# A second feature pass as seven quadrant products, with its input combined ahead of time

## The reference, cut to what matters

```python
def first_block(x, ...):                      # 2048 tokens, 1024 channels
    mixed = concat([y * silu(z) for y, z in branches])    # 1280 wide
    return x + mixed @ w_out                  # 1280 x 1024

def second_block(x, ...):
    xn = rms_norm(x, norm_g) * (1.0 + sc_x) + sh_x
    p = xn @ w_in                             # 1024 x 3072
    f_in, f_gate, q, k, v, na_gate = split_cols(p, six of 512)
    q = rms_norm(heads(q), q_norm_g)          # over each head's 64 channels
    k = rms_norm(heads(k), k_norm_g)
    f_out = fourier(f_in) * silu(f_gate)
    na_out = neighbourhood_attention(q, k, v, ...) * silu(na_gate)
    return x + g_x * (concat([f_out, na_out]) @ w_out)
```

## Time and profile before

| what | value |
|---|---|
| median of three runs | 3404.44 us |
| profiled execution, its span | 3402.36 us, 3400.6 us |
| PE matmuls, busy | 3111.9 us (92%) |
| PE weight loads, busy | 2445.2 us (72%) |
| DVE, ACT, POOL busy | 1514.0, 941.8, 795.5 us |
| token pass, its matmuls L2166 | 1850.4 to 2112.0 us of the span |
| feature pass 2, its last matmul L691 | starts at 2692.6 us |
| DMA | 390.82 MB, mean 115 GB/s |

### The profile page before, as it was taken

How to read it: one execution, slowest core, us unless ns; L and a number is a source line. 1 busy time by engine, 2 the same in 40 slices (tenths; PEclk the granted TensorE clock), 3 DMA queues, 4 the chain that set the end, 5 groups by cost and what they waited for, 6 DMA issues and landing times. The chain is left out here.

```text
span 3400.6 us, 39668 instructions
## 1 busy us (share of the span) xinstructions
PE 3111.9 (92%) x14503; PEld 2445.2 (72%) x14503; DVE 1514.0 (45%) x2504; ACT 941.8 (28%) x1520; POOL 795.5 (23%) x842
## 2 busy tenths in 40 slices
PE   3799999999988999775998999899999898999899
PEld 2588887888876666553897877677888675666687
DVE  6643333042306666386455222476000145777633
ACT  4422212110112334342222234322011133555400
POOL 5322222111112222265342222011111041000111
PEclk7899999999998999778898999999999998999999
DMA  7534335122243341314102666323211235776475
GB/s 272 184 97 116 102 101 180 61 77 75 75 127 87 90 105 55 90 47 97 43 26 82 200 185 208 109 112 123 74 74 74 99 102 134 155 158 142 112 199 148
DMA packets 325559, 390.82 MB, mean 115 GB/s; under 512 B 93879, under 2 KB 260264, under 8 KB 310696
## 3 DMA queue, kind: packets, MB, share of 16 engines
q1 hardware_dynamic: 320692, 387.11, 39.9%
q10 hardware_dynamic: 4704, 1.59, 0.2%
HBM read 256.77 MB, written 135.79 MB: 115 GB/s over the span
## 5 line engine op out<-in xcount | busy, mean ns | idle before, releaser
L691 PE MATMUL f_psum_out<-f_x_high,f_w_high 128*128 128x512 f32 (+1 forms) x1472 | 573.5, 390 | 18.8 <-DVE f_x_low L668 8.1
L691 PE MATMUL f_psum_out<-f_x_low,f_w_high 128*128 128x512 f32 (+1 forms) x1472 | 569.0, 387 | 0.0
L691 PE MATMUL f_psum_out<-f_x_high,f_w_low 128*128 128x512 f32 (+1 forms) x1472 | 568.6, 386 | 0.0
L691 PEld LDWEIGHTS f_psum_out<-f_x_high,f_w_high 128*128 128x128 f32 x1472 | 279.1, 190 | 77.9 <-issue 15.0
L691 PEld LDWEIGHTS f_psum_out<-f_x_low,f_w_high 128*128 128x128 f32 x1472 | 278.9, 189 | 56.5 <-issue 1.7
L691 PEld LDWEIGHTS f_psum_out<-f_x_high,f_w_low 128*128 128x128 f32 x1472 | 278.9, 189 | 55.5
L1351 PE MATMUL nbr_psum_o<-nbr_probT,nbr_v 128*128 128x512 f32 (+3 forms) x576 | 235.8, 490 | 0.0
L683 POOL CAST f_w_high<-f_w 128x1024 fp32r<-128x1024 f32 x41 | 42.6, 1040 | 747.8 <-PE f_psum_out L691 550.5
L532 PE MATMUL p_psum_proj<-p_w_high,p_h_high 128*128 128x512 f32 x512 | 207.5, 405 | 7.4 <-issue 4.0
L532 PE MATMUL p_psum_proj<-p_w_low,p_h_high 128*128 128x512 f32 x512 | 202.1, 395 | 0.0
L532 PE MATMUL p_psum_proj<-p_w_high,p_h_low 128*128 128x512 f32 x512 | 202.1, 395 | 0.0
(11 more groups left out here) (541 smaller groups left out, 6134.0 us busy)
## 6 DMA issues: line engine op xcount, KB each, us to landing
f_w<-in_w_fm SPq DMA_DIRECT2D x45, 512.0 KB, 5.7
side_ada_w<-in_w_ada_rows SPq DMA_DIRECT2D x24, 512.0 KB, 5.7
scratch_qkmT<-p_qkT_out SPq DMA_DIRECT2D x32, 384.0 KB, 4.6
scratch_z1T<-f_out SPq DMA_DIRECT2D x10, 1024.0 KB, 4.8
p_z<-scratch_z1T SPq DMA_DIRECT2D x16, 640.0 KB, 6.6
p_xt<-in_x SPq DMA_DIRECT2D x16, 512.0 KB, 3.9
p_staging<-in_w_tok SPq DMA_DIRECT2D x8, 1024.0 KB, 8.0
scratch_hT<-p_h_slot SPq DMA_DIRECT2D x16, 512.0 KB, 3.3
```

The lines of the kernel that those rows point to most:

```text
L691: last = nc.tensor.matmul(self.p_out[b][:, n * BANK + lo:n * BANK + hi], self.w_parts[b][w_part][:, k, :], self.x_parts[x_part][:, n, k, l ...
```

## The change: what it does

**Quadrants.** The 1024 input channels and the output are cut in two each, and the tokens too: the even tiles form one half of the columns, the odd tiles the other. A pair of output blocks is a 2x2 matrix A of 128x512 quadrants, the input a 2x2 matrix B. A pair now needs seven products of quadrants (Winograd's form of Strassen's scheme) instead of eight. Four of the left operands are sums of weight quadrants (`add_weights`, POOL), four of the right operands are sums of input quadrants (`combine`). DVE adds the seven products to the four results (`merge`).

**Input.** The scratch tensor x2T becomes x2q, with the seven right operands side by side: three quadrants (`move`) and four combinations, which `combine` makes on POOL for each pair of tiles and SP stores in the pair that follows (`move_combined`); for the last pair DVE fills the slot and combines. `fill` now waits also until the combinations of the pair before are stored.

**Pass.** The tokens go in two halves of 1024, and each half walks the 12 pairs in the order `F2_ORDER`, 24 items in all. An item is 7 products of 4 channel blocks by three passes, 84 matmuls of 128x512, into six PSUM banks used in rotation; two banks are left for the sums of squares and v's transposes (`aside`). The seven right operands (1 MB each) are held for a half and loaded anew for the second. There is one buffer for each of the seven split left operands; it is refilled for the next item when its product is done. The weights of item n+2 are loaded as item n begins.

**Roots.** The sums of squares of two heads are two rows of 1024. They are stored to DRAM and loaded as 128x16, ACT takes the root, DVE the reciprocal, and they go by DRAM again to be broadcast over 64 partitions each (`spread_sums`).

**The edge.** Before the last pair of tiles, SP, ACT, POOL and DVE begin with item 0's weights and first operand; before the last tile with the next operands. The second to last tile is transposed inside the last tile's matmuls. PE makes products 0 to 5 of item 0 before the barrier.

```diff
+class QuadrantPass:
+    A11, A12, A22, S1, S2, S3, S4 = range(7)
+    B11, B21, B22, T1, T2, T3, T4 = range(7)
+    PRODUCTS = ((A11, B11), (S2, T2), (A12, B21), (S3, T3), (A22, T4), (S1, T1), (S4, B22))
+    N, HK, BANKS = 7, KB // 2, 6
...
+    def load_w(self, sp, n):
+        if n >= 2:
+            sp.wait_ge(self.a_ready, self.N * (n - 1))
...
+    def load_x(self, sp, half, i):
+        if half:
+            sp.wait_ge(self.prod_ready, self.N * (half * self.per_half - 1) + i + 1)
...
+    def add_weights(self, pool, n):
...
+        pool.wait_ge(self.w_in[n % 2], 16 * (n // 2 + 1))
+        pool.drain()
+        nc.gpsimd.tensor_tensor(s1, a21, a22, ALU.add)
+        nc.gpsimd.tensor_tensor(s3, a11, a21, ALU.subtract)
+        pool.drain()
+        nc.gpsimd.tensor_tensor(s2, s1, a11, ALU.subtract)
+        pool.drain()
+        nc.gpsimd.tensor_tensor(s4, a12, s2, ALU.subtract).then_inc(self.sums_ready, 1)
...
+    def round_w(self, act, n, i):
+        a = self.PRODUCTS[i][0]
+        if n:
+            act.wait_ge(self.prod_ready, self.N * (n - 1) + i + 1)
+        if a < self.S1:
+            act.wait_ge(self.w_in[n % 2], 16 * (n // 2 + 1))
+        else:
+            act.wait_ge(self.sums_ready, n + 1)
+        self.nc.scalar.activation(self.a_high[:, i], self.quadrant(n, a), ACT.Copy).then_inc(self.a_rounded, 1)
+    def rest_of_w(self, pool, n, i):
+        pool.wait_ge(self.a_rounded, self.N * n + i + 1)
+        self.nc.gpsimd.tensor_tensor(self.a_low[:, i], self.quadrant(n, self.PRODUCTS[i][0]), self.a_high[:, i], ALU.subtract)\
+            .then_inc(self.a_ready, 1)
...
+    def product(self, pe, n, i):
+        pe.wait_ge(self.a_ready, self.N * n + i + 1)
+        if n % self.per_half == 0:
+            pe.wait_ge(self.x_ready[i], n // self.per_half + 1)
+        if self.N * n + i >= self.BANKS:
+            pe.wait_ge(self.prod_free, self.N * n + i + 1 - self.BANKS)
...
+        for k in range(self.HK):
+            for at, (w_part, x_part) in enumerate(PASSES):
+                last = self.nc.tensor.matmul(self.bank(n, i), a_parts[w_part][:, i, k, :], x_parts[x_part][:, k, :],
+                                             start=(k == 0 and at == 0), stop=(k == self.HK - 1 and at == len(PASSES) - 1))
+        last.then_inc(self.prod_ready, 1)
...
+    def combine(eng, ops, j):
+        b11, b21, b12, b22 = (slot[b][:, k:k + HK] for b in range(2) for k in (0, HK))
+        t1, t2, t3, t4 = (combined[:, n] for n in range(4))
+        eng.wait_ge(combined_stored, 16 * (j + 1))
+        ops.tensor_tensor(t1, b12, b11, ALU.subtract)
+        ops.tensor_tensor(t3, b22, b12, ALU.subtract)
+        eng.drain()
+        ops.tensor_tensor(t2, b22, t1, ALU.subtract)
+        eng.drain()
+        ops.tensor_tensor(t4, t2, b21, ALU.subtract)
+        eng.drain().then_inc(combined_ready, 1)
...
+                if b == 0:
+                    sp.dma_start(d["x2q"][:, 0:KB, of_pair], slot[0][:]).then_inc(slot_stored[0], 16)
+                else:
+                    sp.dma_start(d["x2q"][:, KB:KB + HK, of_pair], slot[1][:, HK:]).then_inc(slot_stored[1], 16)
+            def move_combined(j):
+                wait_apart(sp, combined_ready, j + 1, taken)
+                sp.dma_start(d["x2q"][:, KB + HK:, bass.ds(j * P, P)], combined[:].rearrange("p s k c -> p (s k) c"))\
+                    .then_inc(combined_stored, 16)
...
+                if b == 1 and not second:
+                    move_combined(j - 1)
...
+            def begin_next():
+                sp.wait_ge(w_ready, MB)
                 for b in range(2):
-                    fp.load(sp, d["w_fm2"], 0, b)
-            def begin_next():
+                    sp.wait_ge(slot_stored[b], 16 * (NT // 4 + 1))
+                sp.wait_ge(combined_stored, 16 * (NT // 4 + 1))
+                fp.load_w(sp, 0)
+                fp.load_x(sp, 0, 0)
+            def go_on():
+                sp.wait_ge(mix_ready[1], PAIRS)
+                sp.wait_ge(o_ready, NT - 1)
+                fp.load_x(sp, 0, 1)
                 sp.wait_ge(slices_used, 1)
-                fp.load_input(sp, d["x2T"], 0, 2)
-                sp.wait_ge(x1_ready[1], PAIRS)
-                fp.load_input(sp, d["x2T"], 2, 3)
+                fp.load_x(sp, 0, 2)
+                fp.load_x(sp, 0, 3)
+                sp.wait_ge(slices_used, 2)
+                fp.load_x(sp, 0, 4)
+                fp.load_x(sp, 0, 5)
...
-            tiles(sp, tile, next_weights, begin_next)
+            tiles(sp, tile, begin_next, go_on)
+            sp.wait_ge(o_ready, NT)
+            fp.load_x(sp, 0, 6)
+            fp.load_w(sp, 1)
             move(PAIRS - 1, 1)
-            sp.wait_ge(slot_stored[0], 16 * (PAIRS + 1))
-            fp.load_input(sp, d["x2T"], 3, 4)
-            sp.wait_ge(slot_stored[1], 16 * (PAIRS + 1))
-            fp.load_input(sp, d["x2T"], 4, 5)
+            move_combined(PAIRS - 1)
...
+                    if last and b == 1 and k == TURN_AT:
+                        turn_x(NT - 2)
+                    if last and b == 1 and k in (SLICES_LENT - 1, 2 * SLICES_LENT - 1):
...
+            for i in range(fp.BANKS):
+                if i == 4:
+                    pe.wait_ge(x_filled, NT)
+                fp.product(pe, 0, i)
+                if i == 1:
+                    turn_x(NT - 1)
...
+                act.wait_ge(combined_stored, 16 * (j + 1))
...
             def begin_next():
-                for b in range(2):
-                    fp.round_first_weights(nc, act, b)
-                fp.round_input(nc, act, 0, 2)
+                fp.round_x(act, 0, 0)
+                for i in range(fp.N):
+                    fp.round_w(act, 0, i)
+            def go_on():
+                fp.round_x(act, 0, 1)
+                fill(PAIRS - 1, 0)
+                fp.round_x(act, 0, 2)
+                fp.round_x(act, 0, 3)
...
-            tiles(act, tile, before_last=begin_next)
-            fill(PAIRS - 1, 1)
-            fp.round_input(nc, act, 2)
+            tiles(act, tile, begin_next, go_on)
+            for i in range(4, fp.N):
+                fp.round_x(act, 0, i)
...
+                if b == 0 and not first:
+                    wait_apart(pool, x_filled, 2 * j, taken)
+                    combine(pool, nc.gpsimd, j - 1)
             def begin_next():
-                for b in range(2):
-                    fp.rest_of_first_weights(nc, pool, b)
+                fp.add_weights(pool, 0)
+                for i in range(fp.N):
+                    fp.rest_of_w(pool, 0, i)
...
-            tiles(pool, tile, before_last=begin_next)
+            tiles(pool, tile, begin_next)
...
+            def begin_next():
+                fp.rest_of_x(dve, nc.vector, 0, 0)
+            def go_on():
+                fp.rest_of_x(dve, nc.vector, 0, 1)
+                fp.rest_of_x(dve, nc.vector, 0, 2)
+            tiles(dve, tile, begin_next, go_on)
...
+            dve.wait_ge(xT_ready, NT)
+            dve.wait_ge(slot_stored[1], 16 * PAIRS)
+            dve.wait_ge(combined_stored, 16 * PAIRS)
+            for k in range(KB):
+                nc.vector.tensor_scalar(slot[1][:, k, :], p_x[:, k, :], g.scale_x[:, k:k + 1], g.shift_x[:, k:k + 1], ALU.mult, ALU.add)
+            dve.drain().then_inc(x_filled, 1)
+            dve.wait_ge(x_filled, NT)
+            combine(dve, nc.vector, PAIRS - 1)
+            for i in range(5, fp.N):
+                fp.rest_of_x(dve, nc.vector, 0, i)
...
+F2_ORDER = (0, 4, 1, 5, 2, 6, 3, 7, 8, 9, 10, 11)
...
+            def spread_sums(n):
+                at = 2 * among(n, "qk")
+                for b in (1, 0):
+                    sp.wait_ge(rows_ready[b], at // 2 + 1)
+                    sp.dma_start(d["rms_in"][at + b], work[b][0:2, :]).then_inc(rows_stored[b], 16)
+                for b in (1, 0):
+                    sp.wait_ge(rows_stored[b], 16 * (at // 2 + 1))
+                    sp.dma_start(spread[b][:], d["rms_in"][at + b].rearrange("h (q c) -> (h q) c", q=HD)).then_inc(spread_in[b], 16)
+                for b in (1, 0):
+                    sp.wait_ge(rms_ready[b], at // 2 + 1)
+                    sp.dma_start(d["rms_out"][at + b].rearrange("h (q c) -> (h q) c", q=HD), spread[b][:]).then_inc(rms_stored[b], 16)
+                for b in (1, 0):
+                    sp.wait_ge(rms_stored[b], 16 * (at // 2 + 1))
+                    for h in range(2):
+                        sp.dma_start(work[b][h * HD:(h + 1) * HD, :], d["rms_out"][at + b, h].partition_broadcast(HD)).then_inc(rms_in[b], 16)
...
+            for n in range(LAST + 1):
+                if n + 2 <= LAST:
+                    fp.load_w(sp, n + 2)
+                if kind(n - 1) == "qk":
+                    spread_sums(n - 1)
+                if kind(n - 1) in ("qk", "v"):
+                    store(n - 1)
+                if n == fp.per_half - 1:
+                    for i in range(N):
+                        fp.load_x(sp, 1, i)
+                if kind(n) in ("in", "gate"):
```

(57 more changed lines are left out.)

368 lines of the change are left out of this document (223 added, 145 removed).

## The result

| | before | changed |
|---|---|---|
| median, us | 3403.52 (8 runs) | 3414.27 (8 runs) |
| lowest and highest | 3399.15, 3406.69 | 3411.70, 3417.54 |
| span of the profiled execution | 3400.6 | 3415.8 |
| PE's first product after the barrier | 2153.34 | 2159.56 |
| last matmul of the pass starts | 2692.61 | 2707.08 |

The ratio is 1.0035, its interval 1.0024 to 1.0045: slower, where 3359 was forecast with 0.92 on faster. The last two rows of the table say where. From PE's resumption (its first product after the barrier) to the pass's last matmul it is 547.5 us now and was 539.3: 8.2 us more with 264 matmuls fewer. The forecast for the same stretch was -59.7 + 3.6 + 4 + 1 = -51.1. So 59.3 us are missing there; the edge came out as forecast (+6.2 for +6.8).

What follows compares the result with a forecast made beforehand. TensorE (PE) was taken as the bound, matmuls times pace in the feature pass. Terms -59.7 + 4 + 1 + 6.8 + 3.6 + 0 - 1 gave -45.3 us, so 3359 us against the median, range 3341 to 3388.

Steps and rivals of the forecast that it cites:

- The edge: Between token and feature pass: reordered queues idle PE about 9 and 17 us, so PE resumes after the barrier +6.8 us later.
- The matmuls removed: Feature pass after the barrier: 264 fewer matmuls at 0.226 us each, -59.7 us if PE stays fed.
- (D): Rival, products: one takes over 2.71 us though PE is fed, gain shrinks 1.6 us per 0.01; (D) and the rest 0.05.
- The roots by DRAM and the six banks: q and k items: the roots' chain frees PE's bank with 1 to 3 us cover; 0.5 us for each of eight, +4.
- (B): Rival, q and k items: chain of roots outruns the six banks; 3387, or 3400 with DVE late; chance 0.28.
- Feeding by POOL: Steady items: POOL's eleven instructions at 1.2 us (upper end 1.77) take about 14 to 17 us, beside PE's 19.0.
- (C): Rival, items: POOL becomes the bound above about 1.85 us per instruction, kernel slower from 2.05; chance 0.05, with similar stalls.
- POOL after the ones: Before item 1: POOL makes four sums and one low part, 6.3 us, while product 6 covers 2.7; +3.6 us.
- The second half's input: Item 11 onward: seven operands loaded anew, last low part about when PE wants it; +1 us, between 0 and 8.
- (A): Rival, edge: pair 6's combinations land early and the 17 us wait goes; about 3342 us, chance 0.12.
- The sum: Whole kernel: all terms give -45.3 us, 3357.1 from the profiled execution, 3359 against the median.

Runs made afterwards that it cites:

- experiment 8: Changed kernel with roots after product 3, merge 0 into u3, the reordered edge, and item 1's sums on POOL before the barrier: 3342.46 us, ratio 0.9836.
- Experiments 1 and 3: Each against the changed kernel: 1 moves roots and reciprocals from product 5 to product 3, 3365.20 us; 3 cuts POOL's low parts to 128 columns, 3361.71 us.
- experiments 6 and 7: Changed kernel, roots after product 3: 6 makes pair 6's combinations on DVE, stored earlier, 3353.89 us; 7 also puts tile 14's work first, 3346.11 us.
- experiment 2: Changed kernel without the sums' way by DRAM, roots and reciprocals (result differs): 3360.43 us in one run.

## Why the prediction was wrong, step by step

- **The matmuls removed, -59.7:** right. Products run at 0.226 to 0.23 us per matmul wherever PE is fed, and the kernel of experiment 8 needs 485.5 us for what took 539.3, 53.8 less, with sums, transposes and the second half's stalls in it. (D) is out.
- **The roots by DRAM and the six banks, +4:** this failed. It was rival (B), though not by its main cause: the hops took the short value (1.5 to 1.6 us for 8 KB, 4.6 for the broadcasts), and the reciprocals came 0.8 us from forecast. The store of the roots, a hop that writes DRAM, took 1.5 us in the median and 3.2 at most, so the late completion that (B) feared for such writes was not seen beyond that. The norm was priced with 1.2, 0.6 and 1.15 us from the earlier trace rows, and took 2.05, 1.63 and 2.13. The rows do not show it, but the trace of the kernel before does: POOL was idle through all eight of the casts from which the 0.6 was halved. In the changed kernel POOL works in every item, so the price was one of another situation. The 0.5 us of wait for each item was taken and not worked out, though the text beside it says that each microsecond beyond the cover costs 8. With a cover (the time by which the last store was to land before PE wants the bank) of 1 to 3 us, 4.7 us more on DVE gave waits of 3.5 to 6.0 us. Experiments 1 and 3 each take away one side of this, and both bring the time to 3362 to 3365, near the forecast of 3359.
- **No clock in that term:** the prediction priced the clock behind the long wait at the edge (1.6 us; 1.3 us measured there) and not in the items. Each wait brought 1.5 to 2.9 us of slow matmuls with it, 17.9 us for the eight, and over the stretch the loss is 18.6 us above that of the kernel before. For this reason, and because DVE was late by more than the 1 to 2 us it allowed, (B), put at 3387 to 3400, came at 3414, among the times that had been given a chance of 0.05.
- **Feeding by POOL:** right. L816 takes 1.47 to 1.59 us in the mean, between the bounds 1.2 and 1.77, and POOL never held a steady item: (C) is out. What it held was DVE.
- **POOL after the ones, +3.6:** a wait of 3.8 us, right, with 2.7 us of slow matmuls behind it that were not counted.
- **The second half's input, +1:** PE is idle 2.0 us from 2420 to 2460, within 0 to 8.
- **The edge, +6.8:** +6.2. Idle before the last tile 11.2 us (9.3 forecast), before tile 15's transpose 15.9 (17), and the fill waited 14.8 us for the combinations' store. That the sum is so close is partly luck: PE began the last tile at 2105.45, 2.4 us sooner than forecast, and 2.5 us of slow matmuls behind that idle time, which nothing in the sum stood for, took it back. (A) is out, and experiments 6 and 7 show that these queues and orders were the cause.
- **The sum:** 6.2 at the edge and 8.2 behind it are 14.4; 0.7 from the last matmul to the end, where -1 was forecast. The two profiles differ by 15.2.

What stays open: how the 59 us would split if only the norm's lengths or only the landing were changed beyond what was run; why the same idle time is followed by slow matmuls once and not another time (below); and why the seventh kernel falls 5 us short of its forecast.

## What to carry to other kernels

Where a chain has a cover of a few microseconds, price every link on it as it runs beside the engines that will be busy then, and look for rows of the same form with both engines at work; DVE and POOL slow each other in both directions. A wait on PE can cost its own length and a stretch at half clock behind it, so that here eight waits of 3.5 to 6.0 us and the slow matmuls behind them ate nearly all that an eighth fewer matmuls had saved. And the remedy can be free: moving the roots and reciprocals two products earlier was worth 49 us.

## What the runs showed of the hardware

- A DVE subtraction of 128x1024, both operands in SBUF, took 2.13 us beside POOL's low parts and 1.29 in the mean beside lighter ones; the cast 1.63 and 0.99, a subtraction of 128x512 1.79 beside POOL and 0.69 alone. POOL's own 128x512 instructions took 1.29 us while DVE waited and up to 2.28 beside DVE's norm.
- After the eight idle times of 3.5 to 6.0 us, 7 to 14 of PE's next matmuls in a row started over 0.3 us apart; after idle times up to 2.2 us ahead of a product only the first did. In between it varied: 3.8 us ahead of item 1 were followed by twelve slow starts in the changed kernel and by one in experiment 2.
- DMAs of 8 KB landed after 1.5 us (to DRAM) and 1.6 us (from DRAM), medians of 16 each.
